# A network of three blocks in float32: x ahead of the weights, and TensorE's split operands at multiples of 1024 bytes

## The reference

```python
# first block, two layers
h = h + mamba2_mixer(rmsnorm(h, g0), ...)        # 1024 -> 5152, depthwise conv, chunked state space, 2048 -> 1024
h = h + conv_glu_ffn(rmsnorm(h, f0), ...)        # 1024 -> 2 x 2816, conv of 3 taps, silu gate, 2816 -> 1024
h = h + fox_attention(rmsnorm(h, g1), ...)       # 16 heads of 64, forget gates, output gate
h = h + conv_glu_ffn(rmsnorm(h, f1), ...)
h = rmsnorm(h, final)
# second block: 16 meta tokens ahead of the 256
h = concat(meta, h)
h = h + concat(mla(...), conv_group(...)) @ w_out   # latent attention, 8 heads; conv of 31 taps over 512 channels
h = h + peer_ffn(rmsnorm(h, ...))                # product keys, 16 of 16384 experts per head, 8 heads
out = rmsnorm(h)[:, 16:272]
```

## Time and profile before

| | us |
|---|---|
| median of 3 runs | 1841.47 (1838.16 to 1842.31) |
| the profiled execution | 1840.81 |
| its span, first to last instruction | 1839.1 |
| TensorE busy | 1729.6 (94%) |
| VectorE, ScalarE, GpSimd busy | 1077.2, 816.3, 912.5 |
| mean granted clock of TensorE | 0.970 |

### The profile page before, as it was taken

The page is one execution under the profiler, slowest core; times in us unless marked ns, Lnnn a source line. Parts: engine busy times, 40 slices in busy tenths (PEclk is TensorE's granted clock), DMA queues, the critical chain, the costliest instruction groups (busy, mean ns, idle before and its releaser), DMA issues. The chain is left out here.

```text
span 1839.1 us, 34906 instructions
## 1 busy us (share of the span) xinstructions
PE 1729.6 (94%) x12587; PEld 1624.0 (88%) x12587; DVE 1077.2 (59%) x2193; ACT 816.3 (44%) x1111; POOL 912.5 (50%) x268
## 2 busy tenths in 40 slices
PE   5879999999999999999988899699999999999996
PEld 5879899999998899999677899699999978888885
DVE  5776756334353563345886880944545277777775
ACT  3446534333646543344434544444444433333332
POOL 3553476887683378886103588956666600000000
PEclk9889999999998999999988999999999999999998
DMA  5442244555453145554103466545545687777774
GB/s 181 138 138 92 92 138 161 184 182 184 162 186 113 48 159 191 183 195 171 68 1 104 141 229 232 186 151 178 185 171 175 214 263 235 239 237 237 238 236 140
DMA packets 77436, 310.78 MB, mean 169 GB/s; under 512 B 8752, under 2 KB 10288, under 8 KB 60720
## 3 DMA queue, kind: packets, MB, share of 16 engines
q1 hardware_dynamic: 74288, 304.64, 49.2%
q10 hardware_dynamic: 3072, 5.09, 0.8%
HBM read 290.82 MB, written 18.87 MB: 168 GB/s over the span
## 5 line engine op out<-in xcount | busy, mean ns | idle before, releaser
L722 POOL TENSOR_TENSOR lo<-raw,hi 128x2048 fp32r<-128x2048 f32 x128 | 588.8, 4610 | 411.8 <-ACT hi L563 338.3
L342 PE MATMUL ps<-xh,hi 128*128 128x256 f32 (+1 forms) x1984 | 569.7, 287 | 38.0 <-POOL lo L722 22.3
L343 PE MATMUL ps<-xl,hi 128*128 128x256 f32 (+1 forms) x1984 | 560.8, 283 | 0.0
L344 PE MATMUL ps<-xh,lo 128*128 128x256 f32 (+1 forms) x1984 | 560.7, 283 | 0.0
L342 PEld LDWEIGHTS ps<-xh,hi 128*128 128x128 f32 x1984 | 378.8, 191 | 41.6 <-issue 31.2
L744 POOL TENSOR_TENSOR lo<-raw,hi 128x1024 fp32r<-128x1024 f32 x128 | 321.4, 2535 | 138.5 <-ACT hi L1686 138.5
L344 PEld LDWEIGHTS ps<-xh,lo 128*128 128x128 f32 x1984 | 378.5, 191 | 0.0
L343 PEld LDWEIGHTS ps<-xl,hi 128*128 128x128 f32 x1984 | 377.9, 190 | 0.2
L1686 ACT ACTIVATE hi<-raw 128x1024 fp32r<-128x1024 f32 x256 | 264.4, 1057 | 214.7 <-PE ps L344 204.8
L2343 DVE TENSOR_TENSOR lo<-raw,hi 128x1024 fp32r<-128x1024 f32 x128 | 156.2, 1222 | 86.0 <-ACT hi L1686 86.0
L342 PE MATMUL ps<-hi,wgh 128*128 128x512 f32 x512 | 201.1, 393 | 1.1 <-DVE wgl L2354 1.1
(11 more groups left out here) (449 smaller groups left out, 3192.3 us busy)
## 6 DMA issues: line engine op xcount, KB each, us to landing
raw<-in_w_u SPq DMA_DIRECT2D x128, 512.0 KB, 4.2
raw<-in_w_v SPq DMA_DIRECT2D x128, 512.0 KB, 4.3
raw<-in_w_up SPq DMA_DIRECT2D x44, 1024.0 KB, 4.8
raw<-in_w_down SPq DMA_DIRECT2D x22, 1024.0 KB, 4.8
raw<-in_w_fox SPq DMA_DIRECT2D x16, 1024.0 KB, 5.0
act_save<-act_out SPq DMA_DIRECT2D x64, 256.0 KB, 2.0
act_in<-act_save SPq DMA_DIRECT2D x64, 256.0 KB, 3.2
raw<-in_w_xbc SPq DMA_DIRECT2D x12, 1024.0 KB, 5.0
```

Source lines behind the costliest of these rows:

```text
L342: pe.matmul(o, ah, bh, start=start, stop=False)
L343: pe.matmul(o, ah, bl, start=False, stop=False)
L344: return pe.matmul(o, al, bh, start=False, stop=stop)
L722: return g.tensor_tensor(lo[slot][:], raw[slot][:], hi[slot][:].bitcast(F32), ALU.subtract)
```

## The change

The order of the tensors is changed so that raw, hi and lo of all three slots, `oh`, `ol`, `hdh`, `hdl`, `xdh` and `xdl` start at multiples of 1024. The normed input gets views `xc` and `xcl` of 8 rows of 256 columns in the space of `xh` and `xl`, also at multiples of 1024; only the third block, which needs the meta columns in front, uses `xh` and `xl` with rows of 272 still. The split meta columns are kept in `xmh` and `xml` until then, and ScalarE copies them into place. wgh0 and wgl0 stay at 0, wgh1 and wgl1 now start at 0 too. In the opening, two quarters of x go first on SP's queue, `w_dt`, `cols` and `rows` move to SP's queue between the units, and ScalarE runs a dummy activation before it waits for x. VectorE makes the low part of unit 0 and splits `w_dt` before it adds up the squares. TensorE's first unit is written out: in its first half the 16 matmuls that need only the high part come before the eight that need the low one.

```diff
     raw, hi, lo = [], [], []
+    ident = sb("ident", [P, P])
+    iota = sb("iota", [P, P])
+    stat = sb("stat", [P, 128])
+    rs = sb("rs", [P, 3, 32])
...
     xh_at = place["at"]
     xh = sb("xh", [P, KC, T2], F32R)
+    xl_at = place["at"]
     xl = sb("xl", [P, KC, T2], F32R)
...
+    xc = sb("xc", [P, KC, SEQ], F32R, at=xh_at)
+    xcl = sb("xcl", [P, KC, SEQ], F32R, at=xl_at + KC * META * 4)
...
-    phase = place["at"]
+    phase = place["at"] = (place["at"] + 1023) // 1024 * 1024
...
-    fcv = sb("fcv", [P, SEQ])
     hdh = sb("hdh", [P, 4, SEQ], F32R)
     hdl = sb("hdl", [P, 4, SEQ], F32R)
+    fcv = sb("fcv", [P, SEQ])
...
+    hm_at = place["at"]
     hm = sb("hm", [P, KC, META])
     hmt = sb("hmt", [P, KC, META])
+    xmh = sb("xmh", [P, KC, META], F32R)
+    xml = sb("xml", [P, KC, META], F32R, at=hm_at)
...
-        xh_, xl_ = x or (xh[:, :, c0:c0 + n], xl[:, :, c0:c0 + n])
+        xh_, xl_ = x or (xc[:], xcl[:])
...
-        run(U_BC, "w_xbc", range(12))
+        def x_quarter(q):
+            sp.dma_start(h[:, 2 * q:2 * q + 2, :], A["x_t"][:, 2 * q:2 * q + 2, :]).then_inc(x_loaded[q], 16)
+
+        x_quarter(0)
+        x_quarter(1)
+        load(0, A["w_xbc"][0], 0)
+        sp.dma_start(wdt[:], A["w_dt"]).then_inc(wdt_loaded, 16)
+        load(1, A["w_xbc"][1], 0)
+        sp.dma_start(cols[:, KC:], A["cols"][:, KC:]).then_inc(cols_loaded, 16)
+        sp.dma_start(rows[:], A["rows"][0].partition_broadcast(P)).then_inc(rows_loaded, 16)
+        load(2, A["w_xbc"][2], 0)
+        run(U_BC + RING, "w_xbc", range(RING, 12))
...
-        lows(0, U_PEER)
+        pool.wait_ge(lo_done, 1)
+        lows(1, U_PEER)
...
+        def first_unit():
+
+            wh, wl = cv3(hi[0][:]), cv3(lo[0][:])
+            pe.wait_ge(hi_done, 1)
+            for k in range(KC):
+                if k % 2 == 0:
+                    pe.wait_ge(x_ready, k // 2 + 1)
+                pe.matmul(ps[:, 0, 0:SEQ], wh[:, k, 0:P], xc[:, k, :], start=k == 0, stop=False)
+                pe.matmul(ps[:, 0, 0:SEQ], wh[:, k, 0:P], xcl[:, k, :], start=False, stop=False)
+            pe.wait_ge(lo_done, 1)
+            for k in range(KC):
+                pe.matmul(ps[:, 0, 0:SEQ], wl[:, k, 0:P], xc[:, k, :], start=False, stop=k == KC - 1)
+            for k in range(KC):
+                if k == 4:
+                    pe_squares(pe, 0, True, True)
+                m = three(pe, ps[:, 0, SEQ:2 * SEQ], wh[:, k, P:2 * P], wl[:, k, P:2 * P], xc[:, k, :], xcl[:, k, :],
+                          k == 0, k == KC - 1)
+            m.then_inc(unit_used, 1)
...
-        for q in range(4):
+        for q in (2, 3):
             act.dma_start(h[:, 2 * q:2 * q + 2, :], A["x_t"][:, 2 * q:2 * q + 2, :]).then_inc(x_loaded[q], 16)
-        act.dma_start(cols[:, KC:], A["cols"][:, KC:]).then_inc(cols_loaded, 16)
-        act.dma_start(wdt[:], A["w_dt"]).then_inc(wdt_loaded, 16)
-        act.dma_start(rows[:], A["rows"][0].partition_broadcast(P)).then_inc(rows_loaded, 16)
+        act.wait_ge(pool_c, 3)
+        s.activation(dtv[:, 8, 0, 0:1], ones[:, 0:1], ACT.Copy)
...
-            if u == 0:
-                for q in range(4):
+            if u < 2:
+                for q in (2 * u, 2 * u + 1):
                     act_square(act, q, 0, h[:, 2 * q:2 * q + 2, :].rearrange("p a b -> p (a b)"))
...
             square(3)
+            s.activation(xh[:, :, 0:META], xmh[:], ACT.Copy)
+            s.activation(xl[:, :, 0:META], xml[:], ACT.Copy)
             act_after(act, U_FFN1 + FFN_UNITS - 1)
...
-            dve_acc(v, 0)
+            v.wait_ge(hi_done, 1)
+            v.tensor_tensor(lo[0][:], raw[0][:], hi[0][:].bitcast(F32), ALU.subtract).then_inc(lo_done, 1)
             v.wait_ge(wdt_loaded, 16)
             ch(v.tensor_copy(wdth[:], wdt[:]))
             sig_v(v.tensor_tensor(wdtl[:], wdt[:], wdth[:].bitcast(F32), ALU.subtract), dt_split)
+            dve_acc(v, 0)
```

More of the change, by code:

```diff
@@ L155, in build @@
     xh = sb("xh", [P, KC, T2], F32R)
+    xl_at = place["at"]
     xl = sb("xl", [P, KC, T2], F32R)
[L157 to L160, removed]
+    xc = sb("xc", [P, KC, SEQ], F32R, at=xh_at)
+    xcl = sb("xcl", [P, KC, SEQ], F32R, at=xl_at + KC * META * 4)
     reuse_at = place["at"]
+    raw.append(sb("raw2", [P, UNIT]))
+    hi.append(sb("hi2", [P, UNIT], F32R))
+    lo.append(sb("lo2", [P, UNIT], F32R))
+    h = sb("h", [P, KC, SEQ])
+    acc = sb("acc", [P, 2, SEQ])
+    xn_at = place["at"]
+    xn = sb("xn", [P, NT, D])
+    oh = sb("oh", [P, 2, 2, SEQ], F32R)
+    ol = sb("ol", [P, 2, 2, SEQ], F32R)
+    tmp = [sb(f"tmp{i}", [P, 512]) for i in range(4)]
     ones = sb("ones", [P, P])
@@ L166, in build @@
     cols = sb("cols", [P, NCOLS])
[L168 to L172, removed]
     rrow = sb("rrow", [P, T2])
@@ L358, in pe_a, with pe_b @@
         m.then_inc(unit_used, 1)
-    def pe_b(pe, s, outs, width=256, ready=None, middle=None):
+    def pe_b(pe, s, outs, width=256, x=None, ready=None, middle=None):
         wh, wl = cv3(hi[s][:]), cv3(lo[s][:])
-        for i, (o, c, m_) in enumerate(outs):
+        for i, (o, c, m_, *other) in enumerate(outs):
+            xh_, xl_ = other[0] if other else x or (xc, xcl)
             if middle is not None and i == 1:
@@ L790, in ssd @@
             for u in range(12):
[L791 to L795, removed]
+                if u == 0:
+                    first_unit()
+                else:
+                    unit_wait(pe, u)
+                    if u >= 2:
+                        pe.wait_ge(xbc_conv, u - 1)
+                    pe_a(pe, u % RING, [ps[:, u % 2, 0:SEQ], ps[:, u % 2, SEQ:2 * SEQ]])
                 if u == 1:
@@ L815, in z_unit @@
                     pe.wait_ge(z_evac, n - 1)
-                pe_b(pe, (U_Z + n) % RING, [(ps[:, n % 2, t * 256:(t + 1) * 256], META + t * P, P) for t in range(NT)])
+                pe_b(pe, (U_Z + n) % RING, [(ps[:, n % 2, t * 256:(t + 1) * 256], t * P, P) for t in range(NT)])
             def rowbc(i):
@@ L968, in fox @@
                     turn(0)
-                pe_b(pe, (U_FQ + n) % RING, [(ps[:, n % 2, t * 256:(t + 1) * 256], META + t * P, P) for t in range(NT)],
+                pe_b(pe, (U_FQ + n) % RING, [(ps[:, n % 2, t * 256:(t + 1) * 256], t * P, P) for t in range(NT)],
                      ready=8 if n == 0 else None, middle=first_heads if n == 15 else None)
@@ L1034, in square_sums @@
                 m.then_inc(ssq_mm, 1)
[L1036 removed]
+            pe_b(pe, U_CQ % RING, [(ps[:, 0, t * 256:(t + 1) * 256], META + t * P, P) for t in range(NT)], x=(xh, xl), ready=16,
                  middle=square_sums)
             unit_wait(pe, U_CKV)
[L1039 to L1040 removed]
+            pe_b(pe, U_CKV % RING, [(ps[0:META, 1, 0:160], 0, META, (xmh, xml))] +
+                 [(ps[:, 1, (1 + t) * 160:(2 + t) * 160], META + t * P, P) for t in range(NT)], width=160, x=(xh, xl))
             def conv_unit(n):
@@ L1666, in routing @@
                         for c in (2 * q, 2 * q + 1):
-                            ins = s.activation(xh[:, c, META:], new_h(c), ACT.Copy)
+                            ins = s.activation(xc[:, c, :], new_h(c), ACT.Copy)
                         ins.then_inc(x_hi, 1)
```

36 lines of the change are left out of this document (18 added, 18 removed).

## The result

| | us |
|---|---|
| after, median of 20 runs | 1843.67 |
| before, median of 20 runs on the same chips | 1841.26 |
| ratio, 95% interval | 1.0016 [1.0009, 1.0023] |
| span of the profiled execution after (before 1839.1) | 1843.9 |

The change did not save 45 us: the kernel is a hair slower, by less than the 0.2% named as the bound of no change. One of the 20 executions after ran in a slower state (granted clock 0.69, 2303.8 us) and is left out of the ratio; the slowest of the others took 1846.3.

The account below looks back on a forecast made before the run. The prediction took TensorE, busy nearly throughout the expert stretches, to bound the kernel, with matmul pace set by operand places. Layout 34.5 us plus head 10.4 made 44.9, taking 1841.5 to 1796 us; range 1784 to 1832.

Parts of the forecast that it names:

- both at the same place: All split operands at 0 within 1024 bytes: 113.9 ns for 256 columns and 227.5 for 512 taken for all.
- `xh` as moving operand: Normed input as moving operand: 11.8 us saved on 2688 matmuls, 10.6 on 2784 in the first expert matrix.
- as stationary operand: Units with the input as stationary operand: 1200 matmuls save 4.3 ns each, 5.2 us.
- The second expert matrix: Half of its 1536 matmuls drop from 232.9 to 227.5 ns, saving 4.1 us.
- The reading behind it: On TensorE, moving operand and next weights don't clash when their places within 1024 bytes keep one good relation; layout saves 34.5 us.
- The head: Opening: TensorE starts at about 11.5 us instead of 22.3; gain 10.4 us, between 6 and 12.5.
- The places do nothing: Rival on the layout: paces differ for another reason, only the head's gain stays, 1831 us; chance 0.13.
- A lower floor: Rival on matmul pace: 111 and 222 ns give 1763 us, the Trainium skill's figures 1738; chance 0.10.
- Multiples of 1024 collide: Rival on the layout: every 256-column matmul takes 119.5 ns, 22 us lost, 10.4 won, 1853 us; chance 0.07.
- The hinge: Over some 10,200 matmuls: a mean pace up by more than 1.0 ns outweighs the head's 10.4 us.
- One sign of being wrong: Expert stretches: the forecast is wrong if GpSimd or the DMA queue appears as TensorE's releaser; no size given.
- that reading of the six pairs: First expert matrix, pairs 20 to 25: faster TensorE only waits longer for VectorE, beyond 8.17 us; 288 matmuls save nothing.

Follow-up runs that it names:

- e3: Changed kernel, other places: slots and wgh0 at 0 past a multiple of 1024, x 64, oh 128, hdh 192, xdh 256, wgh1 64; 1825.71 us, before 1839.66.
- e8: Changed kernel, other places: slots and wgh0 at 0, x 160, oh 32, hdh 224, xdh 96, wgh1 160; 1844.69 us, before 1840.63.
- e2: Changed kernel with the opening of the kernel before, so the new places alone; 1854.79 us, ratio 1.0091 to the kernel before.
- e6: Changed kernel with all inputs, slots, wgh0 and wgh1 at 192 past a multiple of 1024; 1844.54 us, before 1840.63.
- e5: Changed kernel with x, oh, hdh and xdh at 192, slots, wgh0 and wgh1 at 0; 1807.64 us, ratio 0.9818 to the kernel before.
- e9: The kernel of e5 executed once more, unchanged; 1808.35 us, before 1840.67.
- e10: Changed kernel with x, oh, hdh and xdh at 32, slots, wgh0 and wgh1 at 0; 1824.23 us, before 1840.67.

## Why the prediction was wrong

**The step that failed** is the choice of the row for "both at the same place": "The nearest row ... is the odd pairs of the earlier trace rows, 227.5 with their edges, and for 256 columns the 114.0 of the earlier trace rows. I take 113.9 and 227.5 for all." The odd pairs do have distance 0, and their 227.5 is what the new pairs took (226.7). But the 114.0 belongs to a distance of 192. The two rows were joined because one is nearly half of the other, and that is chance. At 2.4 GHz, 120.0 ns is 288 cycles and 226.7 is 544: in both cases the columns and 32 more. The good pace of 256 columns, 113.3, is 272 cycles, the columns and 16. Per matmul the addition at distance 0 is 13.3 ns at both lengths, so halving a 512-column step halves the addition with it and gives 6.6 too little.

**Term by term**, from the table of paces: `xh` as moving operand was to save 22.4 us and cost 11.2; as stationary operand, 5.2 saved, 2.0 lost; `hdh` 1.6 saved, 5.0 lost; `oh` 1.2 saved, 3.6 lost. The second expert matrix was to save 4.1 and saved 5.3: the one term taken from a row with its own distance and its own length is the one with the right sign.

**The reading behind it** was half right. The pace depends on the relation of the two places ("one relation, and a good one"): shown by e3 to e8, and places that differ by a multiple of 256 count as the same. That an equal relation is a good one was not shown by any row for 256 columns, and my bound upward (115 in the forecast's own range) came from the same halving.

**The head.** Forecast at 11.5 for TensorE's start, measured 12.43; gain 9.9 at the start, term 10.4. e1, with the opening alone, gives 11 ± 3 at the end. x's last quarter was the late one (9.62, forecast 6 to 7) and ScalarE's split waited 1.98 for it; the splits themselves, ahead of time, hid most of that. `wdtl` took 0.42 instead of the 4.68 of the earlier trace rows, now that GpSimd stood idle until 15.32. By the Trainium skill, page SBUF — State Buffer, section Who interferes with whom, a VectorE instruction with two SBUF inputs contends with a GpSimd instruction that reads SBUF; the trace agrees. e1 and e2 test it: with the new opening and the old places (e1) it takes 0.42 again, with the old opening and the new places (e2), beside GpSimd's subtraction from 17.48 on, it takes 4.68:
```profile
17.48 13.83 POOL L729 TENSOR_TENSOR lo<-raw,hi 128x2048 fp32r<-128x2048 f32 x3 [13.83 <-ACT hi L1345]
...
22.19 4.68 DVE L1786 TENSOR_TENSOR wdtl<-wdt,wdth 128x256 fp32r<-128x256 f32 x1
```
So it is the order of work, and not the places, that made it short.

**The rivals.** "The places do nothing" (1831) fell with e2. "A lower floor" fell: no 256-column pace held through a run of matmuls was under 113.3. "Multiples of 1024 collide" (1853) had the right sign and nearly the right pace (119.5), but for a wrong reason: e6 has no operand at such a multiple and the same 120.0. It also had the odd pairs slow down by 5.4, and they were the only ones to have had the right distance already; that and the price of the even pairs make up most of the 9 us by which it was too high. Its 0.07 was too small: with one row for distance 0, at another length, the split between it and the forecast should have been near even.

**The hinge** named for the sign, a mean pace up by 1.0 ns, was right: the mean over `xh` rose by 1.9 and the others by 2 to 5, the second expert matrix gave some back, and the result lies just past the point. One sign of being wrong could not tell: "GpSimd ... appears as the releaser of TensorE in the expert stretches" was so before the change (10.6 us). And the wait before the lists was to grow with a faster TensorE; it was 8.14 and 8.15 in e5 and e9, where TensorE was faster, so that reading of the six pairs isn't borne out either.

By the Trainium skill, page TensorE: Matmul & The Clock Gate, section Back-to-back issue gap, the gap between isolated matmuls follows from the columns alone; its formula gives 109.2 ns for 256 at the upper level and 215.8 for 512. No pace of these kinds reached either, and equal columns differ by 6.7 ns with the places alone.

**What stays open.** Why a distance adds what it adds, and what chooses between 113.3 and 117.8. A clash between the reads of the moving operand and those of the next weights is how I read it; the runs show only that the distance decides which paces there are, and that a pace taken at a break in the stream then holds. As the next weights always lie at the same place modulo 256 as the present ones in e3 to e10, these runs can't say which of the two the moving operand must keep its distance from. Distances 32, 64 and 160 for 512 columns, and anything finer than 32 bytes, were not tried.

## What to carry to other kernels

Where a kernel is a dense stream of weight loads and matmuls, read steps from start to start, not mean durations, and note for each stream the distance of its moving and stationary operands modulo 256 bytes; then give the inputs places until it is a good one (here 192 for 256 float32r columns, though it ran at 117.8 in part, and 0 for 512; 0 and 96 were the slowest for 256). Give a term of the sum only the price of a row with the same relation and the same length; a price that was halved or doubled to fit is a guess, and its range has to say so. Put the parts of a change that have nothing to do with each other into separate runs: here a gain of 0.6% was hidden by a loss of 0.9%.

## What the runs showed that I had not expected

The step of a 256-column float32r matmul with its own weights ranges from 113.3 to 120.0 ns by the two places alone; over some 9,000 such matmuls this was worth 36 us between e5 and the kernel after, in 1.8 ms. The best distance for one length is not the best for another: 192 gives 113.3 for 256 columns and 233 for 512, 0 gives 120.0 and 226.7. And a stream can hold either of two paces, 113.3 or 117.8, for a whole stage and take the other one in the next execution of the same program. The five runs of e5 spread over 8.3 us (1802.62 to 1810.93); that this is the cause of the spread is likely but not shown, as only one of the five has a trace.
